# A two-layer diffusion backbone on one core: overflow block loaded early, merge on TensorE, first modulation kept on the chip, SwiGLU reordered

## The reference, cut to what matters

```python
mod = (c_act @ w_ada[l] + b_ada[l])[:, None, :]        # six parts of 1024
sh_a, sc_a, g_a, sh_f, sc_f, g_f = jnp.split(mod, 6, axis=-1)
...
# hier_moe: every token goes to 2 of 32 experts
def expert_block(args):                                 # 128 rows of one expert
    xblk, e = args
    return (jax.nn.silu(xblk @ w_gate[e]) * (xblk @ w_up[e])) @ w_down[e]
...
out = jnp.zeros((t + 1, d), yb.dtype).at[row_tok].add(yb * row_w[:, None])
...
x = layer_norm(alpha * x + g_f * f_lat, ln2_g[l], ln2_b[l])
```

## Time and profile before

| | |
|---|---|
| median of 3 runs | 3427.69 us |
| the profiled execution | 3430.53 us |
| its span | 3428.7 us |
| TensorE busy | 2965.8 us (86%) |
| VectorE busy | 1975.3 us (58%) |
| ScalarE busy | 1382.4 us (40%) |
| GpSimd (POOL) busy | 443.7 us (13%) |
| moved by DMA | 660.35 MB, mean 193 GB/s |
| mean granted TensorE clock | 0.931 of 2.4 GHz |

### The profile page before, as it was taken

How to read it: one execution, slowest core, us unless ns; L and a number is a source line. 1 busy time by engine, 2 the same in 40 slices (tenths; PEclk the granted TensorE clock), 3 DMA queues, 4 the chain that set the end, 5 groups by cost and what they waited for, 6 DMA issues and landing times.

```text
span 3428.7 us, 37077 instructions
## 1 busy us (share of the span) xinstructions
PE 2965.8 (86%) x13288; PEld 2049.5 (60%) x13288; DVE 1975.3 (58%) x2479; ACT 1382.4 (40%) x1672; POOL 443.7 (13%) x453
## 2 busy tenths in 40 slices
PE   4999898899988699999964499898998689999992
PEld 1545356677754577777741245356665467777771
DVE  1781466411125688988843771356121678888885
ACT  0210135411102477777730210146110267777771
POOL 1220000011115200000001420000111410000002
PEclk7999899999998799999987699999999789999996
DMA  7661000221121799999965451002432299999993
GB/s 253 233 183 34 5 1 10 73 66 51 37 106 53 247 392 393 392 392 392 392 235 184 149 179 34 5 1 38 113 86 106 86 329 391 392 393 391 393 379 111
DMA packets 379622, 660.35 MB, mean 193 GB/s; under 512 B 63002, under 2 KB 114634, under 8 KB 379122
## 3 DMA queue, kind: packets, MB, share of 16 engines
q1 hardware_dynamic: 344182, 537.05, 45.0%
q0 software_dynamic: 25824, 87.18, 7.6%
q10 hardware_dynamic: 9504, 34.61, 2.5%
HBM read 610.30 MB, written 51.31 MB: 193 GB/s over the span
## 4 chain that ended last, share of the span: by engine, by line
PE 67%; DVE 10%; ACT 9%; issue 7%; DMA 3%; POOL 1%; DVEq 1%; SPq 0%; PEldq 0%; ACTq 0%; POOLq 0%
PE slot L879 22%; PE abank L760 10%; PE abank L534 7%; PE vbank L767 6%; PE slot L810 4%; ACT round L1679 4%; PE vbank L587 2%; PE abank L560 2%; PE vbank L572 2%; PE slot L637 2%; DVE round L1376 2%; ACT arena L1580 1%; DVE arena L1387 1%; PE vbank L618 1%; PE vbank L506 1%
## 5 line engine op out<-in xcount | busy, mean ns | idle before, releaser
L879 PE MATMUL slot<-round,round 128*128 128x512 f32 x4608 | 1111.4, 397 | 69.1 <-DVE round L1376 65.2
L879 PEld LDWEIGHTS slot<-round,round 128*128 128x128 f32 x4608 | 859.9, 190 | 270.6 <-issue 61.7
L1368 DVE TENSOR_TENSOR round<-arena,round 128x2048 fp32r<-128x2048 f32 x384 | 873.7, 2289 | 157.1 <-ACT round L1679 157.1
L1679 ACT CAST round<-arena 128x2048 fp32r<-128x2048 f32 x384 | 734.4, 1914 | 333.0 <-PE slot L879 302.5
L760 PE MATMUL abank<-round,round 128*128 128x512 f32 (+1 forms) x1728 | 371.1, 371 | 12.1 <-DMA arena<-in_w_o_mla 12.1
L760 PEld LDWEIGHTS abank<-round,round 128*128 128x128 f32 x1728 | 292.0, 191 | 80.0 <-issue 35.1
L534 PE MATMUL abank<-arena 128*128 128x512 f32 (+1 forms) x640 | 227.2, 515 | 3.4 <-ACT arena L1499 3.4
L1630 ACT ACTIVATE arena<-abank,bT 128x512 f32<-128x512 f32 x72 | 44.4, 617 | 457.7 <-PE abank L760 457.7
L1033 DVE SCALAR_TENSOR_TENSOR arena<-arena,csT 128x512 f32<-128x512 f32 x320 | 213.3, 735 | 17.0 <-DMA y_slots<-arena 12.3
L767 PE MATMUL vbank<-arena 128*128 128x512 f32 (+1 forms) x576 | 217.9, 521 | 0.0
L1893 POOL DMA_INDIRECT arena<-h_rows,ids x64 | 79.4, 1241 | 1038.2 <-PE vbank L870 989.5
(11 more groups left out here) (237 smaller groups left out, 3336.8 us busy)
## 6 DMA issues: line engine op xcount, KB each, us to landing
arena<-in_w_gate_e SPq DMA_DIRECT2D x128, 1024.0 KB, 9.6
arena<-in_w_up_e SPq DMA_DIRECT2D x128, 1024.0 KB, 9.6
arena<-in_w_down_e SPq DMA_DIRECT2D x128, 1024.0 KB, 9.6
arena<-in_w_ada POOLq DMA_DIRECT2D x80, 512.0 KB, 4.1
y_slots<-arena ACTq DMA_DIRECT2D x66, 512.0 KB, 6.4
arena<-in_w_in SPq DMA_DIRECT2D x48, 512.0 KB, 6.2
arena<-in_w_in SPq DMA_DIRECT2D x8, 2048.0 KB, 10.0
arena<-in_w_ada SPq DMA_DIRECT2D x4, 2048.0 KB, 16.5
```

The lines of the kernel that those rows point to most:

```text
L879: last = pe.matmul(out_ap, st_, w[:, k, :], start=(first and k == 0 and m == 0), stop=(final and k == 3 and m == 2))
L1368: dve.tensor_tensor(wlo[n0 % RING][:, :, :], raw[n0 % RAW][:, :, :], whi[n0 % RING][:, :, :].bitcast(F32), ALU.subtract).then_inc(lo_ready, 1)
L1679: act.copy(whi[n0 % RING][:, :, :], raw[n0 % RAW][:, :, :]).then_inc(hi_ready, 1)
```

## The change

- **First modulation.** All four `w_ada` chunks have buffers of their own and are the first loads behind the constants, ahead of the bias rows, the input bias and `x`. TensorE's wait for the input bias stays ahead of its products. The trip by DRAM goes: 16 small products transpose `mod_sb` straight into PSUM. SP's loads of the first two `w_in` chunks wait for the products of `w_ada` chunks 1 and 2.
- **Experts.** `SW` is split. The multiply with the gate half (`swish`) stands between `lower(n0 + 6)` and `lower(n0 + 7)`; the multiply with the up half (`swish_up`) stands behind `XTl`. TensorE's gate products wait for `swish` alone.
- **Overflow blocks.** There are two buffer sets. Block 0 stands ahead of the loop, and its loads and its gather are issued before the barrier, when the last `lower` is done. The loop has 5 turns of two blocks. The four rows for the norm (`rows2`) are issued behind block 0's loads.
- **Merge and norm.** All tiles have buffers of their own, so POOL issues all gathers at once. VectorE makes two diagonal matrices a tile from the token weights (`share`), ahead of the barrier. TensorE multiplies them with the gathered rows and adds in PSUM. Beside the moments VectorE does four operations of 1024 columns a tile: times the gate row, plus alpha x, minus mean times `ln_g`, times deviation plus `ln_b`. ScalarE has no part in it, and POOL forms no shift.

The diff, cut to its core (the loops of VectorE, ScalarE and POOL over overflow blocks change as TensorE's does):

```diff
@@ layout
-        wg, wu, wd = ar3(32, KD, FE), ar3(48, KD, FE), ar3(64, 4, D)
+        wg, wu, wd = [[ar3(kb + 48 * n, *shape) for n in range(2)] for kb, shape in
+                      ((0, (KD, FE)), (16, (KD, FE)), (32, (4, D)))]
-        yg = [[ar(32, D), ar(36, D)], [ar(40, D), ar(44, D)]]
-        t12 = [ar(48, D), ar(52, D)]
+        yg = [[ar(32 + 8 * n, D), ar(36 + 8 * n, D)] for n in range(NTILES)]
+        t12 = [ar(136 + 4 * n, D) for n in range(NTILES)]
+        share = [[ar(96 + n, P), ar(96 + n, P, P)] for n in range(NTILES)]
@@ tensor, modulation (the input bias is its own step, ahead of it)
                     for j in range(MOD_FIRST):
-                        w = chunk()
+                        pe.wait_ge(first_in[j], 16)
...
-                pe.wait_ge(mod_back, 32 * (L + 1))
-                ps = vec()
-                close(pe.transpose(ps[:, 0:32], mod_rows[0:32, :], ident[0:32, 0:32]), vgroups)
+                    pe.wait_ge(vec_taken, len(vgroups))
+                    ps = vec()
+                    for j in range(16):
+                        last = pe.matmul(ps[:, 2 * j:2 * j + 2], mod_sb[0:2, j * P:(j + 1) * P], ident[0:2, 0:2],
+                                         start=True, stop=True)
+                    close(last, vgroups)
@@ tensor, GU_wait
-                    pe.wait_ge(am_ready, i + EB)
+                    pe.wait_ge(amid, i + EB)
@@ tensor, overflow blocks
-                pe.sem_inc(X["pe"], 4)
-                with pe.Fori(0, NX) as j:
-                    with pe.If(j < count):
+                def extra_block(j, b, it):
+                    with pe.If(count > j):
...
+                pe.sem_inc(X["pe"], 8)
+                extra_block(0, 0, 0)
+                with pe.Fori(0, NX // 2) as turn:
+                    extra_block(turn * 2 + 1, 1, turn)
+                    extra_block(turn * 2 + 2, 0, turn + 1)
                 barrier("pe", pe)
+                if L + 1 < DEPTH:
+                    input_biases(L + 1)
+                pe.wait_ge(share_ready, L + 1)
+                for n in range(nq):
+                    pe.wait_ge(g_in[n], 32 * (1 + sum(n < len(qtiles(k)) for k in range(L))))
+                    if n >= 2:
+                        pe.wait_ge(t_ready, before(L) + n - 1)
+                    for half in range(2):
+                        for k in range(2):
+                            last = pe.matmul(slot[n % 2][:, half * 512:(half + 1) * 512], share[n][k],
+                                             yg[n][k][:, half * 512:(half + 1) * 512], start=(k == 0), stop=(k == 1))
+                    last.then_inc(mixed, 1)
@@ vector, expert step
                     lower(n0 + 6, it)
+                    swish(b, i)
                     lower(n0 + 7, it)
-                    SW(n0 + 3, it, b, i)
                     if turn:
                         XTl(1 - b, i + 1)
+                    swish_up(n0 + 3, it, b, i)
+                    if turn:
                         lower(n0 + 8, it)
@@ vector, ahead of the barrier, and the merge
+                for n in range(nq):
+                    for k in range(2):
+                        last = dve.tensor_scalar(share[n][k], ident, wtok[:, n, k:k + 1], None, ALU.mult)
+                last.then_inc(share_ready, 1)
                 barrier("dve", dve)
...
-                    link(dve.tensor_scalar(T, Y[0], wtok[:, n, 0:1], None, ALU.mult))
-                    dve.scalar_tensor_tensor(T, Y[1], wtok[:, n, 1:2], T, ALU.mult, ALU.add).then_inc(t_ready, 1)
+                    T = t12[n]
+                    dve.wait_ge(mixed, before(L) + n + 1)
+                    dve.tensor_tensor(T, slot[n % 2][:, :], rows2[f"gf{c}"], ALU.mult).then_inc(t_ready, 1)
                     dve.wait_ge(t_ready, before(L) + n + 1)
-                    link(dve.tensor_tensor(T, T, rows2[f"gf{c}"], ALU.mult))
                     link(dve.scalar_tensor_tensor(T, x_sb[:, t, :], ALPHA, T, ALU.mult, ALU.add))
                     moments(T, t, mv).then_inc(stats_ready, 1)
...
+                    link(dve.scalar_tensor_tensor(T, T, mv[:, t, 0:1], rows2["ln_g"], ALU.subtract, ALU.mult))
                     if n + 1 < nq:
                         merge(n + 1)
-                    dve.wait_ge(norm_ready, NB(L) + 2 * nq + n + 1)
-                    link(dve.tensor_tensor(T, T, rows2["ln_g"], ALU.mult))
-                    dve.tensor_tensor(x_sb[:, t, :], T, rows2["ln_b"], ALU.add).then_inc(x_ready, 1)
+                    dve.wait_ge(rstd_ready, RB(L, "s12") + n + 1)
+                    dve.scalar_tensor_tensor(x_sb[:, t, :], T, rstd[:, t:t + 1], rows2["ln_b"], ALU.mult, ALU.add
+                                             ).then_inc(x_ready, 1)
@@ sync, start and the overflow block
+            for j in range(MOD_FIRST):
+                sp.dma_start(first_ada[j], a["w_ada"][0, :, j * 512:(j + 1) * 512].rearrange("(k p) n -> p k n", p=P)
+                             ).then_inc(first_in[j], 16)
             mod_loads(0)
...
+                sp.wait_ge(lo_ready, UNITS * (L + 1))
+                extra_block(0, 0, 0)
                 barrier("sp", sp)
```

More of the change, by code:

```diff
@@ L202, in program @@
         mod_sb = ar(80, MOD_FIRST * 512)
+        first_ada = [ar3(16 * j, KD, 512) for j in range(MOD_FIRST)]
         ada = [ar3(kb, 2, 512) for kb in (104, 113, 117, 121)]
@@ L327, in program @@
         extra = [{k: sem(f"x{n}_{k}") for k in
-                  ("ids", "rows", "wg", "wu", "wd", "pe", "dve", "act", "y", "go", "end")} for n in range(DEPTH)]
+                  ("ids0", "ids1", "rows0", "rows1", "wg0", "wg1", "wu0", "wu1", "wd0", "wd1",
+                   "pe", "dve", "act", "y", "go", "end")} for n in range(DEPTH)]
+        share_ready, mixed = sem("share_ready"), sem("mixed")
         amid2 = [sem("x0_mid"), sem("x1_mid")]
-        g_in = [sem("g_in0"), sem("g_in1")]
+        g_in = [sem(f"g_in{n}") for n in range(NTILES)]
         out_done = sem("out_done")
@@ L402, in NB @@
         def NB(L):
-            return 3 * before(L)
+            return 2 * before(L)
         def ZB(L, stage):
-            return 2 * NTILES * L + 1 + {"h1": 0, "cq": NTILES}[stage]
+            return 2 * NTILES * L + {"h1": 0, "cq": NTILES}[stage]
         def mod_jobs(L):
@@ L437, in program @@
         gate_vec = []
-        CB = [MOD_FIRST + 7 * L for L in range(DEPTH)]
+        CB = [7 * L for L in range(DEPTH)]
         gate_used = []
@@ L510, in _ @@
             pe.wait_ge(consts_in, 16 * NCONST)
+            input_biases(0)
             modulation(0)
@@ L1753, in _ @@
                         act.dma_start(y_d[bass.ds(j * P + XBASE, P), :], yb[0]).then_inc(X["y"], 16)
+                act.sem_inc(X["y"], 16)
+                extra_block(0, 0, 0)
+                with act.Fori(0, NX // 2) as turn:
+                    extra_block(turn * 2 + 1, 1, turn)
+                    extra_block(turn * 2 + 2, 0, turn + 1)
                 barrier("act", act)
-                for n, t in enumerate(qt):
-                    act.wait_ge(rstd_ready, RB(L, "s12") + n + 1)
-                    act.activation(t12[n % 2], t12[n % 2], ACT.Identity, bias=nmr[:, t, 0:1],
-                                   scale=rstd[:, t:t + 1]).then_inc(norm_ready, 1)
                 if L + 1 == DEPTH:
@@ L1912, in _, with extra_block @@
                     rows_of(i)
+                X = extra[L]
+                count = pool.value_load(ctl[0:1, NX:NX + 1], min_val=0, max_val=NX)
+                def extra_block(j, b, it):
+                    with pool.If(count > j):
+                        pool.wait_ge(X[f"ids{b}"], it * 16 + 16)
+                        if not isinstance(j, int):
+                            pool.wait_ge(X["pe"], j * 4 + 1)
+                        pool.sem_inc(X["go"], 1)
+                        pool.indirect_dma_start(
+                            out=xb[b], out_offset=None, in_=h_d[:, :],
+                            in_offset=bass.IndirectOffsetOnAxis(ap=idx_x[:, b:b + 1], axis=0)).then_inc(X[f"rows{b}"], 16)
@@ L1927, in _ @@
                 barrier("pool", pool)
-                def gather(n):
-                    if n >= 2:
-                        pool.wait_ge(t_ready, before(L) + n - 1)
+                for n in range(nq):
                     for k in range(2):
                         pool.indirect_dma_start(
-                            out=yg[n % 2][k], out_offset=None, in_=y_d[:, :],
-                            in_offset=bass.IndirectOffsetOnAxis(ap=dest[:, k, n:n + 1], axis=0)
-                        ).then_inc(g_in[n % 2], 16)
@@ L1939, in _ @@
-                gather(0)
-                gather(1)
-                for n, t in enumerate(qt):
-                    if n >= 1 and n + 1 < nq:
-                        gather(n + 1)
-                    deviation_and_shift(mv[:, t, :], rstd[:, t:t + 1], nmr[:, t, 0:1])
+                            out=yg[n][k], out_offset=None, in_=y_d[:, :],
```

(3 more changed lines are left out.)

147 lines of the change are left out of this document (75 added, 72 removed).

## The result

The kernel after takes 3385.74 us (median of 4 runs, 3381.76 to 3387.65), the kernel before on the same chip 3428.88 (3426.8 to 3432.4): a ratio of 0.9872, 95% interval 0.9855 to 0.9889. The forecast was 3376 in a range of 3350 to 3398. The profiled execution took 3387.62 us, with a span of 3385.8 beside 3428.7 before: 42.9 us less, where the prediction has 54.

What follows compares the result with a forecast made beforehand. Wait chains were taken to bound the start, overflow blocks and merges; in the experts TensorE and loads were both nearly full. Start 9, experts 17, overflow 15, merge 13 sum to 54 us off 3430.5: 3376, range 3350 to 3398.

Steps and rivals of the forecast that it cites:

- start: First modulation: later first product, then no interruptions and a shorter end; next stage at 63.5 instead of 72.5, 9 us.
- experts: Both expert stages: steps shorten until casts meet landings; 6.2 us in the first layer, 11.0 in the second, 17 us.
- overflow: Overflow blocks: block 0 starts at 1769.5 instead of 1782.4, loops 1 us less a layer; 15 us, between 9 and 19.
- merge: Both merges: shorter tiles and fewer waits against a new fill; 9.0 and 4.1 us, 13 us, between 4 and 18.
- the tail: Start, behind TensorE's last product: what follows shrinks from 10.8 us to about 4.5.
- Small rows land early: Rival at the start: products start at 12 and end at 42; 25 us instead of 9, 3360; chance 0.06.
- The slide: Expert stages: what the schedule gains until casts meet landings; with the other terms 6.2 us first layer, 11.0 second.
- the floor: Expert step: the loads' limit, 7.30 MB a step at 392 GB/s, taken as about 18.6 us.
- `GU_wait` no longer ended by VectorE: Sign in the expert step that the forecast is right; no size given.
- loads have room: Rival in the experts: 392 GB/s is no proven ceiling, TensorE binds at 18.0 us; experts give 39, 3354; chance 0.10.
- the fill: Merge: TensorE's four products for tile 0 between the gather and VectorE, 6.9 us new in each layer.
- Slower: Rival in the experts: casts' waits pass to TensorE; decides from a 19.2 us step, 3448 at 19.5; chance 0.04.

Runs made afterwards that it cites:

- Together: Kernel after plus wide gate/up loads, bias rows ahead, late norm rows, guarded overflow loop: 3318.98 us; that kernel with the 32 small column products spread: 3320.01 us.

## Why the prediction was right, and where it was off

The forecast held, by its mechanisms more than by its sizes: in us, start 9 predicted and 2.8 measured, experts 17 and 11.8, overflow 15 and 10.1 (14.0 less 3.9), merge 13 and 18.4, the rest of the kernel nothing and 0.2 more; 54 and 42.9. Three terms came out 5 to 6 us short and one 5 us over, so a part of the total's fit is that they cancel.

**Start.** Right in kind: small rows last in one queue, first product late, no gap behind. Three sizes were off. The products started at 31.6 and not at 29, and ended at 61.7, where they had ended before; what follows took 8.0 us and not 4.5, as the small products alone took 6.2 (5.6 and 3.7 in the kernel with the late norm rows, at full clock). The term that was least argued, the tail, lost most. "Small rows land early" did not happen, but it was the right thing to ask for: put ahead, they gave about 16 us, and the prediction priced the case at 25 - 9 = 16 above the forecast.

**Experts.** The step that the prediction called most doubtful held in kind: faster steps until casts meet landings, then the loads' pace. The faster steps are 17.7 us and not 18.0. The prediction took TensorE's own work from the earlier trace rows as the step less the wait for `XTl`; the run with wide rows shows 17.80 when nothing is late. The slide was over-priced, 6.2 and 11.0 for 4.6 and 7.2. One part of it is that the floor is 18.72 and not "about 18.6", so that 23 middle steps of the first layer were not as fast as before but 0.07 us slower, 1.6 us in all, as much as this layer's term is short. What of the second layer's terms was too large (1.5 us for an earlier stream, 1.4 for the multiplies) stays open. "`GU_wait` no longer ended by VectorE" was wrong: over 1400 to 1700 us TensorE still waits 16 times, 11.8 us, for `XTl`, as its casts are late by the landings.

The reason given for the floor needs one correction. 392 GB/s was not a limit in bytes: with 8 KB rows for two thirds of the units the same window moves 411. It was the DMA engines' time at 2 KB a packet. The Trainium skill ("DMA: Bandwidth & Descriptors", Bandwidth) gives 425 GB/s for 16 MB by one core. No run here reaches that, and the narrow rows stay 8% below it; "loads have room" was therefore false for these loads and became true when their rows grew.

**Overflow.** 12.9 us were put down to issuing before the barrier. TensorE did start 1.1 us behind it, and the barrier did open 3.6 us later behind the last store (6.5 us for 2.9), but half of the gain was the order against the norm rows, which the prediction did not see as a cost of its own. It still had the total right, since it took the start at 1782.4 as it stood in the earlier trace rows, with that cost in it. For the loops it took 1 us off each layer. In the second layer it was 3.9 us more: TensorE's code for a block stands three times now and not once, and one jump waits for a fetch (5.77 us). In the kernel with the merge on VectorE, where no jump waits, the same stretch takes 11.5 us, 1.6 less than before, near the 1 us of the forecast. The prediction counted turns of the loop and no code. The Trainium skill ("Runtime: NRT & Kernel Launch", Instruction fetch mechanics) says that a taken branch to a place outside of what was fetched ahead stalls for a fetch by DMA. The trace agrees with that rule, 5.77 us with the packet in it, and adds that the fetch queues with other transfers, 3.2 of the 5.77; but which branch is hit changed from kernel to kernel, and no run here shows where the limit lies.

**Merge.** VectorE's time from its first pass to its last fell from 57.2 (1862.8 to 1920.0) to 39.3 us in the first layer, 17.9, where the prediction had 16.9; the fill was 6.2 and not 6.9. In the last merge the same span fell from 39.0 to 26.5 us, 12.5, and the fill was 5.9: 6.6 for the predicted 4.1. Tiles stand 6.43 us apart, as forecast at 6.5; TensorE did not pace them, though granted 0.74 and 0.69 of its clock. About half of the 18.4 us is TensorE's (9.1), the other half the early gathers and the fused norm. The cost of the shares, 1 us each, was 2.5 in the first layer and stands in the overflow stretch, and nothing in the second, where TensorE comes later still.

**Slower** fell: a cast that waits 0.1 to 1.2 us for a landing did not make steps longer than 18.72.

## What to carry to other kernels

When an engine's chain and the loads have nearly the same pace, an edit on one side shows only the difference between them, so price both limits and try both edits together. Where the loads set the pace, count packets beside bytes: a layout that gives each partition neighbouring rows was worth as much here (44.5 us) as the whole change, once the other limit was gone. In one queue put the few bytes that somebody waits for ahead of the megabytes: about 16 us here for the bias rows of the modulation, and about 7 for the block's row numbers. Code is such a transfer too, though in another queue: its fetch was 3.2 us shorter without the norm rows in the engines.

## What was not expected of the hardware

- A branch on TensorE in code that is not at hand costs 2.6 us, and 3.8 to 6.3 with 2 MB of rows in the DMA engines; no jump waits in the kernel with the merge on VectorE, whose TensorE code is shorter, nor in the kernels without the new overflow blocks. Instruction fetches go through the same engines as the data.
- The 32 small products at the start take 3.73 us or 5.7 to 6.2, with the same code up to there. The granted clock is the difference. Both windows are of the small products alone, the first of after, the second of the kernel with the bias rows ahead:

```profile
62.90:69.20 6.30, 6.17 (x32) 6.08 (x32) 0.25 (x2) 0.00 (x0) 0.00 (x0) 0.58 0.01 3
```

```profile
46.30:50.20 3.90, 3.73 (x32) 3.64 (x32) 0.25 (x2) 0.00 (x0) 0.00 (x0) 1.00 0.66 233
```

  Before either, TensorE had worked for 30 us and then waited 1.3 us for VectorE's addition. In one it was granted 2.4 GHz on, in the other mostly 1.2; of nine kernels three had the fast form. It moves the whole time by 2.5 us, and the last products of an overflow block by as much (0.70 and 1.00, in the section Together), so a single profile of this kernel is not good to less.
- A packet of 2 KB takes 88 ns and one of 8 KB 313. With narrow rows the loads stop at 392 GB/s; with wide ones they gave the 411 that TensorE asked for, and their own limit was not reached.
